# Weight tiles in pairs of 1 MB, 8 KB per partition, and one row slot fewer

## The reference, cut to what matters

```python
mod = silu(c) @ w_ada + b_ada                       # 6 vectors of 1024: shifts, scales, gates
h = modulate(rms_norm(x, g_mix), sh1, sc1);  proj = h @ w_in
o_sb, o_d = stick_breaking(...), dilated(rope(q_d), rope(k_d), v_d)
x = x + gt1 * ((sigmoid(gate_sb) * (o_sb @ w_sb_o) + sigmoid(gate_d) * (o_d @ w_dil_o)) @ w_out)
h2 = modulate(rms_norm(x, g_ffn), sh2, sc2)
q = h2 @ w_pq                                       # 8 heads; top 16 by two sets of keys
expert, gate = top_k(...)                           # 8 x 16 experts for each token
x = x + gt2 * sum_k gate_k * gelu(h2 . u[expert_k]) * v[expert_k]
x = second_block(rms_norm(x, g_final))              # proj, mixer, attention, ff1, ff2, gate
```

## Time and profile before

| | |
|---|---|
| median of the runs | 1381.94 us (1381.83 to 1382.34) |
| profiled execution, its span | 1379.6 us from the first to the last instruction, 2.3 us less than the median of the runs |
| PE, VectorE, ScalarE, GpSimd busy | 87%, 53%, 24%, 22% of the span |
| bytes moved | 520.11 MB, mean 377 GB/s |
| first gather issued, last gather issued | 189.58 us, 1077.16 us |

### The profile page before, as it was taken

One profiled execution on the slowest core, in us unless ns is written; L12 is line 12 of the kernel. 1 busy time (PEld: TensorE's weight loads), 2 busy tenths in 40 slices (PEclk: granted clock), 3 DMA queues, 4 the chain that ended last, 5 costly groups with the idle time before them and its releaser, 6 DMA issues.

```text
span 1379.6 us, 17021 instructions
## 1 busy us (share of the span) xinstructions
PE 1197.6 (87%) x5984; PEld 614.6 (45%) x5984; DVE 734.8 (53%) x2087; ACT 329.1 (24%) x904; POOL 307.5 (22%) x271
## 2 busy tenths in 40 slices
PE   5999998968877875679889989889877999999998
PEld 4788975535544431232334343323222344544444
DVE  6456467967776775876646555564644332310002
ACT  2412144223211131232223212211111143311102
POOL 0000013434233343433222222222434100000000
PEclk9999999989989987879999999999999999999999
DMA  9999989999999999999999999999999899788882
GB/s 371 405 365 396 391 330 376 418 419 418 418 416 418 408 410 419 386 375 418 416 415 416 416 408 411 415 417 415 417 417 417 313 411 367 223 262 287 290 300 91
DMA packets 107267, 520.11 MB, mean 377 GB/s; under 512 B 12208, under 2 KB 12976, under 8 KB 73904
## 3 DMA queue, kind: packets, MB, share of 16 engines
q0 software_dynamic: 41088, 285.23, 50.8%
q1 hardware_dynamic: 63648, 228.29, 43.7%
q10 hardware_dynamic: 2448, 5.51, 1.1%
HBM read 516.36 MB, written 1.05 MB: 375 GB/s over the span
## 4 chain that ended last, share of the span: by engine, by line
PE 53%; DMA 33%; DVE 7%; ACT 3%; issue 2%; SPq 1%; ACTq 0%; POOL 0%; DVEq 0%; POOLq 0%
PE ps_M L957 26%; DMA ring<-in_w_second 17%; DMA ring<-in_peer_uv,arena 9%; PE ps_T L757 7%; PE ps_M L659 4%; DMA ring<-in_w_pq 2%; DMA arena<-in_peer_uv,arena 2%; PE ps_M L512 2%; PE ps_M L489 2%; DVE ring L2148 1%; PE ps_M L682 1%; DMA arena<-in_w_ada 1%; PE ps_M L718 1%; PE ps_OT L945 1%; DMA merged<-in_peer_uv,arena 1%
## 5 line engine op out<-in xcount | busy, mean ns | idle before, releaser
L957 PE MATMUL ps_M<-ring,arena 128*128 128x512 f32 x1072 | 500.9, 606 | 42.7 <-DMA ring<-in_w_second 42.4
L957 PEld LDWEIGHTS ps_M<-ring,arena 128*128 128x128 f32 x1072 | 191.1, 190 | 308.1 <-issue 234.3
L1272 POOL DMA_INDIRECT ring<-in_peer_uv,arena x137 | 163.5, 1193 | 335.7 <-PE ps_T L760 318.6
L757 PE MATMUL ps_T<-ring,arena 64*64 64x512 f32 x274 | 160.7, 675 | 65.5 <-ACT arena L1408 64.2
L1272 POOL DMA_INDIRECT arena<-in_peer_uv,arena x105 | 121.5, 1157 | 238.5 <-PE ps_T L760 227.7
L760 PE MATMUL ps_T<-ring,arena 64*64 64x512 f32 x274 | 160.7, 675 | 0.0
L759 PE MATMUL ps_T<-ring,arena 64*64 64x512 f32 x274 | 160.7, 675 | 0.0
L758 PE MATMUL ps_T<-ring,arena 64*64 64x512 f32 x274 | 160.7, 675 | 0.0
L757 PE MATMUL ps_T<-arena 64*64 64x512 f32 x210 | 119.8, 656 | 24.3 <-ACT arena L1408 24.2
L1400 ACT ACTIVATE arena<-arena 128x2 f32<-128x2 f32 x128 | 25.8, 202 | 404.8 <-DVE arena L2168 400.5
L760 PE MATMUL ps_T<-arena 64*64 64x512 f32 x210 | 119.8, 657 | 0.0
(11 more groups left out here) (347 smaller groups left out, 1712.7 us busy)
## 6 DMA issues: line engine op xcount, KB each, us to landing
ring<-in_w_second SPq DMA_DIRECT2D x274, 512.0 KB, 4.6
ring<-in_w_in SPq DMA_DIRECT2D x66, 512.0 KB, 12.7
arena<-in_w_ada POOLq DMA_DIRECT2D x8, 2048.0 KB, 16.3
ring<-in_w_pq SPq DMA_DIRECT2D x28, 512.0 KB, 5.6
arena<-in_w_ada SPq DMA_DIRECT2D x16, 512.0 KB, 15.1
ring<-in_w_out SPq DMA_DIRECT2D x16, 512.0 KB, 5.8
ring<-in_w_br SPq DMA_DIRECT2D x16, 384.0 KB, 8.8
ring<-in_peer_uv,arena POOLq DMA_INDIRECT x137
```

The costliest lines, as they stand in the source:

```text
L757: mm(ps["T0"][low, :], d[low, :], row[low, 0:512], start=first, stop=last)
L957: m = mm(bank, left[c], w[:, c, :], start=first and c == 0, stop=last and c == 1)
L1272: pool.indirect_dma_start(row_slots[s], None, A["peer_uv"], bass.IndirectOffsetOnAxis(ap=expert[:, u % 3, k:k + 1], axis=0))\
```

## The change

All weight tiles are laid out on the host in pairs, the two tiles of a pair side by side in each partition (8 KB; the branches' pairs 6 KB), in the order in which they are loaded. SP issues one DMA of 1 MB for each pair, and a slot pair has one semaphore. The ring has 12 slots, six pairs. Rows get ring slots 0 to 5 (`VR` = 6) and not 0 to 7, so there are eight row slots, and six from gather 63 on; weights go round in three pairs (ring slots 6 to 11) beside the gathers. A pair's slots are free when both tiles are used. Both halves of a query are one pair, placed where half 0 stood. `LATE` is 8 tiles in front of the end of the shared stage.

```diff
-RING, OPENING = 13, 12
-OWN, LENT, VR = 3, 2, 8
+RING = 12
+OWN, LENT, VR = 3, 2, 6
-EARLY = 62
+EARLY = 63
-OPENERS, CYCLES = (4, 6, 0, 1, 3, 2, 7, 8), ((4, 6, 0, 1, 3, 2, 7, 8, 5), (6, 0, 1, 2, 7, 8, 5))
+OPENERS, CYCLES = (4, 6, 0, 1, 3, 2, 7), ((4, 6, 0, 1, 3, 2, 7, 5), (0, 1, 6, 7, 5, 2))
...
-    s = (OPENERS + 6 * CYCLES[0])[n] if n < EARLY else CYCLES[1][(n - EARLY) % 7]
+    s = (OPENERS + 7 * CYCLES[0])[n] if n < EARLY else CYCLES[1][(n - EARLY) % len(CYCLES[1])]
...
-        FIRST += [(what, c) for c in range(3)] + [(f"q{u}", 0), (what, 3), (f"q{u}", 1)] + [(what, c) for c in range(4, KC)]
+        FIRST += [(what, c) for c in range(4)] + [(f"q{u}", 0), (f"q{u}", 1)] + [(what, c) for c in range(4, KC)]
...
-for n in range(LEAD + QUARTERS):
+for n in range(0, LEAD + QUARTERS, 2):
+    turns_here = [t for t in TURN_AT[n:n + 2] if t is not None]
+    for t in turns_here:
+        if t // TOPK + NH + 2 < NU and t % TOPK == 5:
+            FIRST += [(f"q{t // TOPK + NH + 2}", half) for half in (0, 1)]
     if n >= LEAD:
-        FIRST.append(("w0", n - LEAD))
-    if TURN_AT[n] is not None:
-        if TURNS // TOPK + NH + 2 < NU and TURNS % TOPK in (5, 7):
-            FIRST.append((f"q{TURNS // TOPK + NH + 2}", TURNS % TOPK // 7))
-        TURNS += 1
+        FIRST += [("w0", n - LEAD), ("w0", n - LEAD + 1)]
+    TURNS += len(turns_here)
...
-LATE = ALONE - 12
+LATE = ALONE - 8
+PAIRS = RING // 2
...
-order = list(range(OPENING))
-for n, name in enumerate(FIRST):
+order = list(range(PAIRS))
+for n in range(0, len(FIRST), 2):
+    pair = FIRST[n:n + 2]
     if n == SHARED:
-        order = [RING - 1] + list(range(VR, RING - 1))
+        order = [4, 5, 3]
     elif n == LATE:
-        by_last_row = sorted(range(VR // 2), key=lambda s: landings[OWN + LENT + s][-1])
-        order = [2 * s + i for s in by_last_row for i in (0, 1)] + order
+        order = sorted(range(VR // 2), key=lambda s: landings[OWN + LENT + s][-1]) + order
...
+        p = order.pop(0)
+        if pair[0] not in KEPT.values():
+            order.append(p)
+        loads[p] += 1
+        BEFORE[pair[0]] = held[p]
+        held[p] = pair[1]
+    for i, name in enumerate(pair):
+        SLOT[name] = (2 * p + i, 16 * loads[p])
...
             def first_tiles(lo, hi):
-                for name in FIRST[lo:hi]:
+                for name in FIRST[lo:hi:2]:
...
-                    to = slots(slot, 1).rearrange("p s c n -> p (s c n)")[:, 0:n]
-                    eng.dma_start(to, src).then_inc(tile_in[slot], 16)
+                    to = slots(slot, 2).rearrange("p s c n -> p (s c n)")[:, 0:n]
+                    eng.dma_start(to, src).then_inc(tile_in[slot // 2], 16)
...
+def in_pairs(tiles, order=None):
+    tiles = tiles[list(range(len(tiles))) if order is None else order]
+    return tiles.reshape(len(tiles) // 2, 2, P, -1).transpose(0, 2, 1, 3).reshape(len(tiles) // 2, P, -1)
```

More of the change, by code:

```diff
@@ L137 @@
 FIRST += [("w1", n) for n in range(QUARTERS) if n not in PLP]
-LATE = ALONE - 12
+LATE = ALONE - 8
+PAIRS = RING // 2
 KEPT = {("q8", half): ("q7", half) for half in (0, 1)}
 SLOT, BEFORE = {}, {}
-loads, held = [0] * (RING + len(GUESTS)), [None] * RING
-order = list(range(OPENING))
-for n, name in enumerate(FIRST):
+loads, held = [0] * (PAIRS + len(GUESTS) // 2), [None] * PAIRS
+order = list(range(PAIRS))
+for n in range(0, len(FIRST), 2):
+    pair = FIRST[n:n + 2]
     if n == SHARED:
-        order = [RING - 1] + list(range(VR, RING - 1))
+        order = [4, 5, 3]
     elif n == LATE:
-        by_last_row = sorted(range(VR // 2), key=lambda s: landings[OWN + LENT + s][-1])
-        order = [2 * s + i for s in by_last_row for i in (0, 1)] + order
[L153 to L170, removed]
+        order = sorted(range(VR // 2), key=lambda s: landings[OWN + LENT + s][-1]) + order
+    if pair[0] in KEPT:
+        p = SLOT[KEPT[pair[0]]][0] // 2
+        order.append(p)
+    elif pair[0] in GUESTS:
+        p = PAIRS + GUESTS.index(pair[0]) // 2
+        loads[p] += 1
+    else:
+        if pair[0] == ("lga", 0):
+            order = [0]
+        p = order.pop(0)
+        if pair[0] not in KEPT.values():
+            order.append(p)
+        loads[p] += 1
+        BEFORE[pair[0]] = held[p]
+        held[p] = pair[1]
+    for i, name in enumerate(pair):
+        SLOT[name] = (2 * p + i, 16 * loads[p])
 (X3_SQ, X3_ROOT, R3, X4_SQ, X4_ROOT, R4, R4H, LN_PART, _, LN_SUM, LN_NEG, LN_SQ, LN_ROOT, LN_INV, X5_SQ, _, X5_SUM, R5,
@@ L373, in build @@
         quarter_done = {}
-        tile_in = [sem(f"tile_in{s}") for s in range(RING + len(GUESTS))]
+        tile_in = [sem(f"tile_in{s}") for s in range(PAIRS + len(GUESTS) // 2)]
         vec_in, ident_in, x_in, key_in, const_in, const2_in = (
@@ L480, in tile @@
                 slot, landed = SLOT[name]
-                pe.wait_ge(tile_in[slot], landed)
+                pe.wait_ge(tile_in[slot // 2], landed)
+                if name[0] in ("br0", "br1"):
+                    both = slots(slot // 2 * 2, 2).rearrange("p s c n -> p (s c n)")
+                    return both[:, slot % 2 * 6 * P:(slot % 2 + 1) * 6 * P].rearrange("p (c n) -> p c n", n=P)
                 return slots(slot, 1)[:, 0]
@@ L1248, in _ @@
             slot, landed = SLOT[STICKS[-1]]
-            pool.wait_ge(tile_in[slot], landed)
+            pool.wait_ge(tile_in[slot // 2], landed)
             pool.wait_ge(first_in[1][KC - 1], 16)
@@ L2710, in quarter_tiles, with in_order @@
     return w.reshape(k // 256, 2, P, n // 512, 512).transpose(3, 0, 2, 1, 4).reshape(n // 512, k // 256, P, 2 * 512)
+def in_pairs(tiles, order=None):
+    tiles = tiles[list(range(len(tiles))) if order is None else order]
+    return tiles.reshape(len(tiles) // 2, 2, P, -1).transpose(0, 2, 1, 3).reshape(len(tiles) // 2, P, -1)
+def in_order():
+    dilated = [12 + 6 * s + 2 * (x % DIL_G) + x // DIL_G for x in range(6) for s in range(2)]
+    return list(range(12)) + dilated + list(range(24, 30)) + [30 + KC * s + c for c in range(KC) for s in range(2)]
 def lay_out(inputs):
@@ L2733, in lay_out @@
         x[name] = x[name][0]
[L2734 to L2735 removed]
+    x["w_in"] = in_pairs(column_tiles(x["w_in"][0]), in_order())
+    for name in ("w_out", "w_pq"):
+        x[name] = in_pairs(column_tiles(x[name][0]))
     x["c"] = x["c"].reshape(D)
     x["w_ada"] = x["w_ada"][0].T.reshape(6 * KC, P, D)
[L2738 removed]
+    x["w_br"] = in_pairs(column_tiles(np.concatenate([x.pop("w_sb_o")[0], x.pop("w_dil_o")[0]], 0)))
     w_in2 = quarter_tiles(x.pop("w_in_2")[0])
```

26 lines of the change are left out of this document (11 added, 15 removed).

## The result

The change makes the kernel slower: 1407.4 us median (1403.7 to 1411.2, 4 runs) against 1381.9, a ratio of 1.018 (95% interval 1.017 to 1.019). The forecast was 1378.7 with a range up to 1388: wrong in sign and outside the range.

What follows compares the result with a forecast made beforehand. Full DMA engines were taken as the bound in 240 to 1070 us, PE before 190 and from 1105 us. Terms -4.5 - 0.2 + 0.9 + 0.3 + 0.3 = -3.2 us took 1381.94 to 1378.7, range 1375 to 1388.

Steps and rivals of the forecast that it cites:

- Order and SP: Shared stage, queries 10 to 15: loads behind a held query pair up to 7.5 us late; cost 0, uncovered at most 45 us.
- The DMA is never empty meanwhile: While SP stands behind a query pair, 11 us of gathers in flight keep the DMA busy; a reason for cost 0.
- 0.8 us spare a turn: Shared stage: PE needs 2.93 us of each 3.77 us turn, so has 0.8 us spare; a reason for cost 0.
- One row slot fewer: Gathers: 0 taken for the shared stage (range 0 to 24 us), +0.9 at the start, +0.3 at 590 us.
- The start's bound of 2.5 us: 190 to 240 us: the lost row slot leaves the DMA one row behind, 0 to +2.5 us; +0.9 taken.
- The stretch around 590 to 620 us: DMA not quite full there, so a prefetching row slot is lost: range 0 to +2.5 us, +0.3 taken.
- Rate: Full DMA, 190 to 1090 us: 8 KB packets make weight bytes 2% cheaper, -4.5 us (bounds 0 and 7.3).
- a microsecond gained or lost before about 1075 us is one at the end: The PE-bound end begins when the last turn is done, so earlier gains or losses count in full.
- Shares: Shared stage: queues served packet for packet, so weights get one half, not one third; gathers become late, no time moved.
- Head: Before the first gather: `w_ada` chunks (-1 to +4.0 us) and rope swap (0 to +2.3) beside 8 KB packets; +0.3 taken.
- The rival of the starved loop: Shared stage: row slots come back too slowly with six, 7.5 us more, 1386.2 us in all; chance 0.21.
- The rival that SP's queue makes no 8 KB packets: Weight loads: no rate or share changes, one slot missing, costs of +1.5 us stand, 1383.4 us; chance 0.10.

Runs made afterwards that it cites:

- e1_deal: The changed kernel with the slots of the pair used up first, not the query's, dealt out first behind queries 10 to 15: 1390.2 us, ratio 1.0053.
- e4_six_singles: The kernel before with only the changed kernel's slots: ring of 12, one row slot fewer, six single 4 KB weight tiles beside the gathers: 1388.9 us, ratio 1.0042.
- e7_nine_then_six: The kernel before, single tiles, with one row slot fewer only from gather 62 on (nine slots, then six): 1387.1 us, ratio 1.0041.
- e12_fourteen: The changed kernel with 14 ring slots, nine then seven row slots, 4 KB opening loads, queries re-placed and re-dealt, keys of only four heads held: 1382.1 us, ratio 1.0000.
- e2: The changed kernel with each pair loaded by two DMAs of 4 KB per partition, still freed and waited for as a pair: 1456.1 us, ratio 1.0534.
- e5: The changed kernel with the edits of e1_deal and e2 together: 1433.2 us, ratio 1.0370.
- e3_wide_ada: The changed kernel with the `w_ada` chunks on the Pool queue in 8 KB runs instead of 4 KB: 1411.4 us, ratio 1.0198.

## Why the prediction was wrong, by its steps

**The step that failed: "Order and SP".** It named the mechanism, the six places, the pair behind which SP stands, and put it at 0, with up to 45 us uncovered. Taking the hold out gives 17 us (e1_deal). Two reasons given for 0 did not hold. "The DMA is never empty meanwhile": 11 us of rows in flight cover a wait of SP only while rows are reissued, and they are reissued by PE, which is what stops. And "0.8 us spare a turn" is no cover for a wait of 4 us. The hold was also taken as two turns, 7.5 us. From the first half's use to the end of the second it was 9.6 to 10.6 us at four of the query pairs and 14.5 at the one of 853.9 us (877.88 to 892.37), and SP stood 13.2 to 26.4 us, as it comes to that load well before PE uses the query. At the first three places the landings show no cost, so there 0 was right; it failed above all at the one of 853.9 us, with some 9 us. (The issues saved are 203 and not 137, 442 against 239 on SP's queue; at a price of 0 that changes nothing.)

**One row slot fewer** was sized 1.2 us in all; e4_six_singles has 0.42%, 6 us. The share in the shared stage was right (0). The start's bound of 2.5 us was too low: a lost row there costs the wait for the next slot, 4 us at gather 8. The stretch around 590 to 620 us, +0.3 in the sum, costs most: the DMA share is 0.95 where the earlier trace rows has 0.99, and e7_nine_then_six puts 0.41% from gather 62 on, all of it by gather 144, which lands at 640 us before.

**Rate**: right as a rate (in 960 to 1060 us 417 GB/s before, 420 in e1_deal, 421 in e12_fourteen; 4.5 us of bytes forecast, 5.0 found), wrong as time. e12_fourteen shows where it is: in weights moved ahead, not in rows.

```profile
DMA packets 5774, 42.04 MB, mean 420 GB/s; under 512 B 645, under 2 KB 645, under 8 KB 645
DMA packets 5764, 42.05 MB, mean 421 GB/s; under 512 B 634, under 2 KB 634, under 8 KB 634
```

That those could have been rows instead is argued, not shown. The same traces show that "a microsecond gained or lost before about 1075 us is one at the end" was too simple. In the kernel before, the last row has been there for 9.4 us when PE comes to it. The last gather lands 28.3, 14.3 and 4.2 us late in the changed kernel, e1_deal and e12_fourteen, where the spans are 22.3 and 8.9 us longer and 0.4 shorter.

**Shares**: right in direction (who is late), though not in size: in 960 to 1060 us SP's queue has 15.73 of 41.26 MB, 38% and not one half, as it waits for slots. The sentence that it moves no time is refuted by e2 and e5: with 4 KB packets the same three pairs are 43 to 49 us slower.

**Head**: +0.3 forecast, +2.1 found at the first gather, inside the swap's bound of 2.3; the trace shows the swap and not the `w_ada` chunks.

Together 17 + 6 + 2 = 25 of 25.5 us, with no gain of the rate to be seen in the time. The 17 and the 6 are runs of their own; the 2 is the first gather's delay, and no run takes it out alone. The rival of the starved loop had the right direction and the right sign to know it by (a share below 1), but priced at 7.5 us what takes 17. The rival that SP's queue makes no 8 KB packets is refuted, for packets as the trace counts them: 34416 packets carry its 228.28 MB, 6.6 KB on average. The 4096 bytes that the Trainium skill (DMA: Bandwidth & Descriptors, "SWDGE vs HWDGE vs iDMA") gives as the preferred bound of a packet do not hold for these.

The 2% taken from the stretches of the earlier trace rows stands up. A third of the bytes of 960 to 1060 us (14.15 of 41.68 MB before) changed their packet size, and the rate rose by 0.7 to 1.0% in all; for those bytes that is 2 to 3%. The overhead rule of the Trainium skill (DMA: Bandwidth & Descriptors, "Why small descriptors are slow"), by which the prediction had an estimate of 1.1% for them, gives less than this trace has.

## What to carry to other kernels

When buffers are merged into pairs, work out for each pair the time from its issue to the last use of its second half, and look at what the fixed order of the queue puts behind it: one pair that mixes near and far uses stops all loads behind it, and a single place where the rows are late as well can cost most of the loss. "The DMA stays busy meanwhile" must be followed to who reissues the transfers; if it is the engine that stops, the cover is gone. A gain in rate on a full queue was no time here: it went to bytes that were not the ones awaited at the end of the stage.

## What the runs showed of the hardware

- Two backed-up queues were served packet for packet (378 against 376 in the earlier trace rows, at twice the bytes), and the packet size set the time to landing: beside gathers a 1 MB pair lands 9.5 us after its issue in 8 KB packets and 12.7 to 13.4 in 4 KB packets; a 512 KB single tile, in the kernel before, takes 14.2, with three or four queued.
- Small packets on a third queue landed later beside larger ones on the others: the swap of 92.85 us came 2.1 us later beside 8 KB packets on one queue, and that of 76.51 us came 1.7 us later beside one such queue, 4.6 us later beside two (e3_wide_ada) and 0.8 us later beside none (e2_two_loads).
- Behind a wait of 3.6 or 4.0 us PE's granted clock was 0.50, that is 1.2 and not 2.4 GHz, over the next 3.6 to 3.8 us, and back at 1.00 within 8 us; before the wait it was 1.00. Behind a wait of 3.32 us (757.71) the next group took 1.98 us, as at full clock.
- A rate on a full DMA: 417 GB/s with 4 KB and 8 KB packets in about equal number, 420 to 421 with 8 KB alone but for the small ones.
